# Query and key products of both mixers as one product of 512 columns, with later turns and a new end of the second mixer

## The reference, cut to what matters

```python
def rmsnorm(x, g):
    y = xf * lax.rsqrt(jnp.mean(xf * xf, axis=-1, keepdims=True) + EPS)
    return (y * g.astype(jnp.float32)).astype(x.dtype)

def dsw_mixer(h, w_qkv, q_gain, k_gain, w_o, rel_bias):
    qkv = (h @ w_qkv).reshape(B, S, 3, G, Hg, HEAD_DIM)
    q = rmsnorm(qkv[:, :, 0], q_gain)
    k = rmsnorm(qkv[:, :, 1], k_gain)
    v = qkv[:, :, 2]
    ...            # per group of 8 heads: windowed attention with a bias, softmax over the three groups
    return o.astype(h.dtype) @ w_o

def moba_mixer(h, w_qkv, q_gain, k_gain, w_o, rel_bias):
    qkv = (h @ w_qkv).reshape(B, S, 3, H, hd)
    q = rmsnorm(qkv[:, :, 0], q_gain).transpose(0, 2, 1, 3)
    k = rmsnorm(qkv[:, :, 1], k_gain).transpose(0, 2, 1, 3)
    ...            # causal attention per head with a bias
    return o.astype(h.dtype) @ w_o

for i in range(DEPTH):     # DEPTH = 2
    u = rmsnorm(h, norm_mix[i])
    h = h + (dsw_mixer if i == 0 else moba_mixer)(u, ...)
    h = h + sq_relu_mlp(rmsnorm(h, norm_ffn[i]), ffn_w1[i], ffn_w2[i])
```

## Time and profile before

| | us |
|---|---|
| median of 3 runs | 1662.42 (1661.85 to 1662.98) |
| profiled execution, its own time | 1662.12 |
| its span | 1660.2 |
| TensorE busy | 1625.4 (98% of the span) |
| VectorE busy | 1240.5 (75%) |
| ScalarE busy | 972.9 (59%) |

### The profile page before, as it was taken

The page is one execution under the profiler, slowest core; times in us unless marked ns, Lnnn a source line. Parts: engine busy times, 40 slices in busy tenths (PEclk is TensorE's granted clock), DMA queues, the critical chain, the costliest instruction groups (busy, mean ns, idle before and its releaser), DMA issues.

```text
span 1660.2 us, 27613 instructions
## 1 busy us (share of the span) xinstructions
PE 1625.4 (98%) x11068; PEld 1478.9 (89%) x11068; DVE 1240.5 (75%) x1766; ACT 972.9 (59%) x1381; POOL 309.5 (19%) x307
## 2 busy tenths in 40 slices
PE   8999999999999999999999999999899999999997
PEld 6988888898888889998999999999898888888886
DVE  5565786665658666998875554799888898988897
ACT  6556675346656634555554443555558677776675
POOL 1331553123217402143120002132120000000000
PEclk9999999999999999999999999999999999999999
DMA  8632545455335554533435444543429898988983
GB/s 294 233 109 101 178 178 203 180 205 175 113 128 192 178 203 181 183 136 131 150 122 187 174 178 178 172 150 128 167 94 343 333 353 335 340 333 331 352 342 127
DMA packets 50197, 339.76 MB, mean 205 GB/s; under 512 B 5575, under 2 KB 7839, under 8 KB 10351
## 3 DMA queue, kind: packets, MB, share of 16 engines
q1 hardware_dynamic: 47344, 328.79, 54.3%
q0 software_dynamic: 2720, 9.13, 1.8%
HBM read 336.76 MB, written 1.13 MB: 204 GB/s over the span
## 4 chain that ended last, share of the span: by engine, by line
PE 88%; DVE 5%; ACT 3%; issue 1%; POOL 1%; DMA 1%; SPq 0%; DVEq 0%; POOLq 0%; ACTq 0%
PE bank L528 12%; PE bank L502 8%; PE bank L504 8%; PE bank L503 8%; PE bank L526 7%; PE bank L956 5%; PE bank L957 5%; PE bank L958 5%; PE bank L659 3%; PE bank L661 3%; PE bank L660 3%; PE bank L989 2%; PE bank L988 2%; PE bank L987 2%; DVE wl L1698 2%
## 5 line engine op out<-in xcount | busy, mean ns | idle before, releaser
L1698 DVE TENSOR_TENSOR wl<-stg,wh 128x2048 fp32r<-128x2048 f32 x310 | 712.4, 2302 | 212.1 <-ACT wh L1198 210.2
L1198 ACT ACTIVATE wh<-stg 128x2048 fp32r<-128x2048 f32 x310 | 592.7, 1912 | 185.6 <-PE bank L958 82.4
L502 PE MATMUL bank<-xx,wh 128*128 128x272 f32 (+1 forms) x810 | 235.2, 290 | 2.5 <-DVE xx L2123 2.5
L504 PE MATMUL bank<-xx,wl 128*128 128x272 f32 (+1 forms) x810 | 232.5, 287 | 0.0
L503 PE MATMUL bank<-xx,wh 128*128 128x272 f32 (+1 forms) x810 | 232.3, 287 | 0.0
L528 PE MATMUL bank<-xx,wh 128*128 128x512 f32 x448 | 159.7, 396 | 0.0
L502 PEld LDWEIGHTS bank<-xx,wh 128*128 128x128 f32 x810 | 152.4, 188 | 5.1 <-issue 3.5
L503 PEld LDWEIGHTS bank<-xx,wh 128*128 128x128 f32 x810 | 153.6, 190 | 0.0
L504 PEld LDWEIGHTS bank<-xx,wl 128*128 128x128 f32 x810 | 152.3, 188 | 0.0
L528 PE MATMUL bank<-H,wh 128*128 128x512 f32 x434 | 151.3, 390 | 0.0
L956 PE MATMUL bank<-wh,GH 128*128 128x512 f32 (+3 forms) x400 | 147.5, 369 | 0.0
(11 more groups left out here) (374 smaller groups left out, 3507.6 us busy)
## 6 DMA issues: line engine op xcount, KB each, us to landing
stg<-in_w SPq DMA_DIRECT2D x310, 1024.0 KB, 4.8
BT<-bias_scratch POOLq DMA_DIRECT2D x3, 1024.0 KB, 11.2
BT<-bias_scratch POOLq DMA_DIRECT2D x1, 2048.0 KB, 13.0
BB<-bias_scratch POOLq DMA_DIRECT2D x2, 1024.0 KB, 6.4
res<-in_x SPq DMA_DIRECT2D x1, 1024.0 KB, 5.8
stg<-in_w SPq DMA_DIRECT2D x2, 512.0 KB, 7.4
BB<-bias_scratch POOLq DMA_DIRECT2D x2, 512.0 KB, 7.1
out<-res SPq DMA_DIRECT2D x4, 256.0 KB, 3.0
```

The lines of the kernel that those rows point to most:

```text
L502: pe.matmul(out, wh, xh(kt), start=kt == 0, stop=False)
L504: ins = pe.matmul(out, wl, xh(kt), start=False, stop=kt == KT - 1)
L1198: act.activation(WH[u % NW][:, :], stg[u % NS][:, :], ACT.Copy).then_inc(*m.inc("w_high", u))
L1698: vec.tensor_tensor(WL[u % NW][:, :], stg[u % NS][:, :], WH[u % NW][:, :].bitcast(F32), ALU.subtract).then_inc(*m.inc("w_low_v", u))
```

## The change

For each group, query and key become one product: `query_key` takes 4 blocks of weights per kt and issues the three matmuls with 512 columns into one bank per token tile, query in columns 0 to 255 and key in 256 to 511. The weights are laid out for it on the host side (`head_tiles`). Half a kt (one token tile) is now one slot, so that slots, units and split points keep their numbers: slot 8 bi + 2 kt + tt. Both kinds are ready only at the end of the key's entry of `order`, so ACT's copies, POOL's squares and DVE's sums come as four tiles in a row behind entry bi of kind 1, and none behind kind 0 (ACT and DVE still split a unit at kt 0 there).

The tables move too. In the first mixer two turns come two slots later, (8, 7) to (9, 1), and one slot later, (16, 7) to (17, 0). In the second mixer all turns move: behind slot 1 of the entry that follows the values, and `order` ends with (3, 0), (3, 1), (2, 2), (3, 2), so that the last two value pairs stand behind the last keys. The plan that follows from these tables for the second mixer is: before, steps 0 to 7 in slots (3, 1) to (4, 7), 8 to 15 in (6, 1) to (7, 7), 16 to 23 in (9, 1) to (10, 7), 24 to 37 left over; after, steps 0 to 6 in (3, 3) to (4, 7) and 7 in (5, 1), 8 to 14 in (6, 3) to (7, 7) and 15 in (8, 1), 16 to 18 in (9, 3) to (9, 7), 19 to 21 in (10, 1) to (10, 5), 22 to 25 in (11, 1) to (11, 7), 26 to 37 left over. In the first mixer the plan stays as it is (steps 2 and 3 in (10, 2) and (10, 5), 4 and 5 in (11, 2) and (11, 5)). The early split ahead of step 26 goes.

```diff
-              turns={(3, 5): 0, (6, 5): 1, (8, 7): 2, (12, 5): 3, (15, 1): 4, (16, 7): 5},
+              turns={(3, 5): 0, (6, 5): 1, (9, 1): 2, (12, 5): 3, (15, 1): 4, (17, 0): 5},
...
-              order=QKV[:12], turns={(3 * gi + 2, 7): gi for gi in range(4)},
-              sums_at=(0, 7), ring=8, late=24, leads={24: 0, 25: 1, 27: 2, 29: 3, 31: 4, 33: 5, 36: 6}, tables={})]
+              order=QKV[:8] + [(3, 0), (3, 1), (2, 2), (3, 2)], turns={(3, 1): 0, (6, 1): 1, (9, 1): 2, (11, 1): 3},
+              sums_at=(0, 7), ring=8, late=24, leads={27: 0, 28: 1, 29: 2, 30: 3, 31: 4, 33: 5, 36: 6}, tables={})]
...
+                def products(out, kt, tt, wh, wl):
+                    pe.matmul(out, xh_t(kt, tt), wh, start=kt == 0, stop=False)
+                    pe.matmul(out, xl_t(kt, tt), wh, start=False, stop=False)
+                    return pe.matmul(out, xh_t(kt, tt), wl, start=False, stop=kt == KD - 1)
+
+                def query_key(bi, gi):
+                    bs = [bank(("qkv", l, gi, 0, tt), ("raw", (l, gi, 0, tt)), ("raw", (l, gi, 1, tt))) for tt in range(2)]
                     held.update(b for b, _ in bs)
                     for kt in range(KD):
-                        wh, wl = take(2)
+                        wh, wl = take(4)
...
+                            ins = products(PS[b][:, :], kt, tt, wh, wl)
...
+                            between(*divmod(bi * KD + 2 * kt + tt, KD))
...
+                for bi, (gi, kind) in enumerate(c["order"]):
+                    if kind == 0:
+                        query_key(bi, gi)
+                    elif kind == 2:
+                        value(bi, gi)
...
-                        ps = bank(("qkv", l, gi, kind, tt))[:, 0:256]
+                        ps = bank(("qkv", l, gi, kind, tt))[:, kind % 2 * 256:kind % 2 * 256 + 256]
...
-                    if l == 0 and bi == 0:
+                    if kind == 0:
                         continue
-                    if l == 0 and bi == 1:
-                        evac(*c["order"][0])
+                    if kind == 1:
+                        evac(gi, 0)
                     evac(gi, kind)
                 for i in rest:
-                    if l == 1 and i == 26:
-                        sp.one_ahead()
                     step(i)
...
-                    for k1 in ((0, 1) if l == 0 and bi == 1 else (kind,) if kind < 2 else ()):
+                    for k1 in ((0, 1) if kind == 1 else ()):
...
-                    if kind < 2:
-                        for tt in range(2):
-                            i = kind * 2 + tt
-                            w.wait_ge(*m.of("raw", (l, gi, kind, tt)))
+                    if kind == 1:
+                        for i in range(4):
+                            k1, tt = divmod(i, 2)
+                            w.wait_ge(*m.of("raw", (l, gi, k1, tt)))
...
```

More of the change, by code:

```diff
@@ L643, in transposes, with between @@
                             ins.then_inc(*m.inc("group", ("qk", l, gi, kind, tt)))
-                for bi, (gi, kind) in enumerate(c["order"]):
-                    sem = "v_out" if kind == 2 else "raw"
-                    bs = [bank(("qkv", l, gi, kind, tt), (sem, (l, gi, kind, tt))) for tt in range(2)]
+                def between(bi, kt):
+                    if (bi, kt) in plan:
+                        step(plan[bi, kt])
+                    if (bi, kt) == c["sums_at"]:
+                        if l == 0:
+                            w.wait_ge(*m.of("consts_in"))
+                        square_sums(st, 2 if l == 0 else 1)
+                    if (bi, kt) in c["tables"]:
+                        bias_table(c["tables"][bi, kt])
+                    if (bi, kt) in c["turns"]:
+                        transposes(c["turns"][bi, kt])
+                def products(out, kt, tt, wh, wl):
[4 more added lines that the diff above has]
+                    bs = [bank(("qkv", l, gi, 0, tt), ("raw", (l, gi, 0, tt)), ("raw", (l, gi, 1, tt))) for tt in range(2)]
                     held.update(b for b, _ in bs)
                     for kt in range(KD):
-                        wh, wl = take(2)
+                        wh, wl = take(4)
                         if bi == 0:
@@ L657, in mixer @@
                                 vacant(old)
[L658 to L661, removed]
+                                m.bank["qkv", l, gi, 1, tt] = b
+                            ins = products(PS[b][:, :], kt, tt, wh, wl)
@@ L662, in mixer @@
                             if kt == KD - 1:
-                                ins.then_inc(*m.inc("group", ("qkv", l, gi, kind, tt)))
+                                ins.then_inc(*m.inc("group", ("qkv", l, gi, 0, tt)))
+                                m.also("group", ("qkv", l, gi, 1, tt))
+                                if tt == 1:
+                                    m.also("group", ("unit", at[0] // UT - 1))
+                            elif tt == 1 and unit_over():
+                                ins.then_inc(*m.inc("group", ("unit", at[0] // UT - 1)))
@@ new lines, in query_key, with value @@
+                            between(*divmod(bi * KD + 2 * kt + tt, KD))
+                    let_go(*sorted(b for b, _ in bs))
+                def value(bi, gi):
+                    bs = [bank(("qkv", l, gi, 2, tt), ("v_out", (l, gi, 2, tt))) for tt in range(2)]
+                    held.update(b for b, _ in bs)
+                    for kt in range(KD):
+                        wh, wl = take(2)
+                        for tt in range(2):
+                            b, old = bs[tt]
+                            if kt == 0:
+                                vacant(old)
+                            ins = products(PS[b][:, 0:256], kt, tt, wh, wl)
+                            if kt == KD - 1:
+                                ins.then_inc(*m.inc("group", ("qkv", l, gi, 2, tt)))
@@ L664, in mixer @@
                         if kt == KD - 1:
                             m.also("group", ("unit", at[0] // UT - 1))
[L666 to L673, removed]
@@ L674, in mixer @@
-                        if (bi, kt) in c["turns"]:
-                            transposes(c["turns"][bi, kt])
-                    let_go(*sorted(b for b, _ in bs))
+                        between(bi, kt)
+                    let_go(*sorted(b for b, _ in bs))
+                for bi, (gi, kind) in enumerate(c["order"]):
[3 more added lines that the diff above has]
+                        value(bi, gi)
                 name, KT, lead, old = f"wo{l}", c["HG"] // 2, [], []
@@ L2465, in mixer @@
                             step(plan[bi, kt])
-                    if kind < 2:
-                        for tt in range(2):
-                            i = kind * 2 + tt
-                            w.wait_ge(*m.of("raw", (l, gi, kind, tt)))
+                    if kind == 1:
+                        for i in range(4):
+                            k1, tt = divmod(i, 2)
+                            w.wait_ge(*m.of("raw", (l, gi, k1, tt)))
                             if gi >= 1:
-                                w.wait_ge(*m.of("head_sum", (l, gi - 1, kind, tt)))
+                                w.wait_ge(*m.of("head_sum", (l, gi - 1, k1, tt)))
                             w.wait_ge(*m.of("rstd", st))
-                            pool.tensor_tensor(sqr[i], raw[i], raw[i], ALU.mult).then_inc(*m.inc("raw_sq", (l, gi, kind, tt)))
+                            pool.tensor_tensor(sqr[i], raw[i], raw[i], ALU.mult).then_inc(*m.inc("raw_sq", (l, gi, k1, tt)))
                     if l == 0 and bi == 3:
@@ L2628, in head_tiles @@
     t = w.reshape(k // P, P, 3, groups, 2, 2, P)
-    return np.concatenate([t[:, :, kind, mixer["groups"][gi][1], mixer["groups"][gi][2]].transpose(0, 2, 1, 3).reshape(-1, P, P)
-                           for gi, kind in mixer["order"]])
+    part = lambda gi, kind: t[:, :, kind, mixer["groups"][gi][1], mixer["groups"][gi][2]].transpose(0, 2, 1, 3)
+    return np.concatenate([(np.concatenate([part(gi, 0), part(gi, 1)], axis=1) if kind == 0 else part(gi, 2)).reshape(-1, P, P)
+                           for gi, kind in mixer["order"] if kind != 1])
 def token_tiles(w):
```

## The result

The changed kernel took 1672.44 us (median of 4 runs, 1670.93 to 1673.13), the kernel before 1662.13 (4 runs) beside it: 1.0064 of the time, 95% interval 1.0053 to 1.0076. That is slower by 0.64%; the prediction was 1675.0 us, in a range of 1665 to 1681.

The account below looks back on a forecast made before the run. TensorE was taken to set the time. Second-mixer waits 14.7, first mixer 1.6 and clock 3.4, less 3.0 at the second mixer's end and 3.8 for columns, gave +12.9 us on 1662.12: 1675.0 us, range 1665 to 1681.

Parts of the forecast that it names:

- The deciding step: Second mixer's products: steps' bias falls behind head norm and split on DVE, so TensorE waits 14.7 us together.
- r: Start of ACT's first copy for the second mixer's head norm, put at K + 1.6 us.
- K: End of a group's last key product in the second mixer; a late step's bias was put at K + 10.4 us.
- The waits, group by group: TensorE's waits in the second mixer: group 1 4.1 us, group 2 3.5, group 3 6.9, group 0 0.2.
- the 0.9 at (11, 3): Second mixer, group 3: the bank of job 22 waits 0.9 us behind a split, some 9 us after the 6.0 wait.
- The columns: Query and key products: 960 matmuls of 256 columns become 480 of 512, saving 3.8 us.
- The first mixer: First mixer: longer norm burst and later turns change TensorE's waits by +1.6 us, bounds 0 and +3.5.
- The end: Second mixer's last steps: waits for QT 0.6 and bias 1.4 go, 1.0 of slow clock too: 3.0 us saved.
- The clock: Second mixer: two slow stretches of 1.7 us each behind long TensorE waits, +3.4 us, bounds 0 and 8.5.
- Rival 2: TensorE's waits come, clock stays up, engines that got ahead save 2 us more: +7.5 us, 1669.6; chance 0.24.
- Rival 3: Each of TensorE's five long waits brings a slow clock stretch of 1.7 us: +18.0 us, 1680.1; chance 0.11.
- Rival 1: Second mixer: TensorE reaches the banks late enough not to feel DVE's chain: -6.8 us, 1655.3; chance 0.08.

Follow-up runs that it names:

- The table of four: Wide-product kernels: turns as before, values as before 1659.65 us or behind the last keys 1659.77; turns two slots later, 1671.40 and 1672.44 (the changed kernel).
- steps at other slots: Changed kernel with the second mixer's steps in slots 1, 3, 4, 6, 7 of an entry in place of 1, 3, 5, 7: 1659.66 us.
- the split twice: Changed kernel with VectorE making the low half of one weight unit twice behind the second mixer's norms of groups 1 to 3: 1680.31 us.
- the kernel with the values back: Changed kernel with the second mixer's values, lead tiles and early split as before, turns still two slots later: 1671.40 us.
- the first four runs: The first four experiments, timed in rounds beside the kernel before, which took 1661.38 us there.

## Why the prediction was right

**The deciding step held.** The links of VectorE's chain came within 0.3 us of what was worked out: r at K + 1.9 (ScalarE's first copy at 433.66) for K + 1.6, the bias at K + 10.6 for K + 10.4. TensorE's own arrival was counted 0.5 to 0.8 us too early: it stands at K + 8.2, 9.2 and 4.9 in groups 1 to 3, for 7.7, 8.4 and 4.4, since the first product behind a step takes 0.1 us more than the others (432.58 to 432.81) and the odd step 0.68 us and not 0.5 (434.11 to 434.79). Moving the bias on VectorE alone took the loss away, and lengthening the chain by 2.3 lengthened the waits by 2.3.

**The waits, group by group.** Group 1: 2.4 and 0.7 for 2.7 and 1.4; group 2: 1.5 and 1.1 for 2.0 and 1.5; group 3: 5.7 for 6.0, and the 0.9 at (11, 3) did not come; group 0: none for 0.2. The sum is 11.4 us where the prediction had 14.7, inside its bounds of 9 to 19. The three long waits were right to 0.5 us. The waits for QT that follow in groups 1 and 2 were too long in the forecast for the same reason as the long ones: ScalarE's last copy ends at 399.28 and 427.50, K + 15.2 and 14.5 for 15.3 and 14.5, but TensorE comes at K + 14.5 and 13.5 for 13.9 and 13.0. Why the 0.9 did not come was not taken apart.

**What caused them** was named half. The prediction gave both table changes as reasons, the late turns and the values behind the last keys. The table of four shows that the turns alone make the loss, whichever place the values have; they only decide at which instruction TensorE then waits.

**The columns.** 480 x (0.235 - 0.229) = 2.9 us by the medians, for 3.8. The three matmuls per tile of the earlier trace rows (0.227) were the nearer form, but 0.002 too fast; nothing comes near the 0.20 us that would have refuted the step. One reading was not right: the view of the earlier trace rows also has two waits for a split of weights, 0.5 us ahead of the first product and 0.3, where the prediction says none. No term rests on it.

**The first mixer.** +1.6 less its share of the columns (288 of 480, 2.3) is -0.7; measured -1.29. With 288 x 0.006 = 1.7 of columns its waits cost 0.4 and not 1.6. The wait for zm behind the norm is there, 1.1 us for 0.8 of before and a predicted 2.0, and the wait for the POOL division fell from 1.6 to 0.7 (11 to 167 us):

```profile
PE bank L581 <- ACT QT L1295: 1.2, 2, 0.8
PE bank L658 <- DVE zm L1801: 1.1, 1, 1.1
...
PE bank L594 <- POOL Lm L2487: 0.7, 1, 0.7
```

With only the products wide its first to last product took 136.18 us, in the changed kernel 135.72. The new turns were not tried alone, and the seven kernels with wide products that have them take 135.48 to 136.06, so that a gain of the turns is not shown. What they change can be read: the wait of 1.3 us for the POOL division at 144.7 us has gone, and two for QT, of 0.4 and 0.8 us, have come.

**The end.** The waits for QT and for the early split's bias went, 2.0 as predicted, and the slow stretch with them. The late split costs nothing that shows. The rest of the 6.04 us by which the end is shorter is work that moved into the products.

**The clock** was mis-sized. Two slow stretches were predicted at 1.7 us each (+3.4), and 1.0 of the one of before to go: +2.4 together. In the mixers there is one, longer, in place of one. PEclk stands third from the end of the row:

```profile
441.00:448.00 7.00, 5.63 (x29) 4.77 (x30) 2.37 (x11) 2.41 (x9) 2.42 (x3) 0.51 0.46 150
```

It is 1.2 GHz from 441 us, within the wait, to 447.9; TensorE works in it for 5.5 us, so that 2.7 are lost, against 1.7 in the earlier trace rows: +1.0 net. A second one, outside the mixers (1185.1 to 1188.5 us), stands behind waits that the kernel before has too, at full clock there. Of the ten profiles of this document five have one at this place (the changed kernel, the wide products alone, the tables alone, steps at other slots, the split twice), five have none: it belongs to the execution and not to the change. It does not cost its 1.7 us either: the part behind the second mixer is 0.56 longer, since two waits of 0.5 us each for ScalarE, which the kernel before has at 1190 and 1191 us, do not come.

**The sum** stood at +12.9 on the profiled execution and +8.8 was measured on it (span to span), +10.3 between the medians. The waits gave 3.3 less, the clock in the mixers 1.4 less, the first mixer 1.2 less, the columns 0.9 less of a gain; that makes 7.9. The two mixers measured +8.45 (9.74 - 1.29), of which a wait of 0.4 for PTm in the products, in no term of the sum, is most of the 0.55 left over; what is left beyond the mixers is mostly the 0.56 behind them, less 0.3 at the start and the end. All terms but the columns err to the same side, so that the sum is not right by errors that cancel. Rival 2 had 1669.6 and its condition, waits at full clock, was met for two of three long waits: the truth lies between forecast and rival 2. The median of 1672.44 is in the forecast's band, the profiled execution, at 1670.93, just outside it, in rival 2's. Rival 3 fell (no slow stretch behind 2.4 and 1.5 us), though with the split made twice every wait for zm had one. Rival 1 fell. The Trainium skill's section cited for rival 3 ("TensorE: Matmul & The Clock Gate", "What's actually happening") holds for the 5.7 us wait, and no more than sometimes for the shorter ones, as the last part shows.

## What to carry to other kernels

A table that places work on one engine also places it in the queues of the others: before a step is moved by a slot or two, look where it falls relative to the longest burst on each in-order engine, for the step that comes behind the burst carries all of it. An engine that is busy for half of a stretch can set the time one for one at such a place, and the cheap repair is to reorder the engine that is late (or to fit the steps ahead of the burst), which here gave back all of the loss. Of the wider product's gain the reordering left 0.2 us at an equal clock, and the steps ahead of the burst 1.5. When a step is moved out of the way, count which one now stands last behind the burst, and who asks for it.

## What the hardware showed beyond that

The clock does not answer to a wait of a given length in the same way each time. In the kernel with the values back, TensorE twice waited 2.38 us in the same place of two groups, after the same last products:

```profile
395.92 0.50 PE L658 MATMUL bank<-wh,xx 128*128 128x512 f32 x1 [2.38 <-DVE zm L1803]
...
424.88 0.70 PE L658 MATMUL bank<-wh,xx 128*128 128x512 f32 x1 [2.38 <-DVE zm L1803]
```

Behind the first the clock stayed at 2.4 GHz, behind the second it fell to 1.2 for 3.4 us:

```profile
396.00:400.00 4.00, 3.82 (x23) 3.14 (x23) 0.94 (x1) 4.00 (x9) 0.93 (x1) 1.00 0.74 262
425.00:429.00 4.00, 4.00 (x17) 3.68 (x18) 0.98 (x1) 4.00 (x9) 0.93 (x1) 0.57 0.73 266
```

Likewise the waits of the earlier trace rows were followed by a slow stretch in the kernel before and by none with the wide products alone, whose window reads 1.00:

```profile
443.50:468.00 24.50, 20.74 (x173) 16.46 (x172) 14.03 (x45) 14.34 (x43) 0.93 (x1) 1.00 0.24 87
```

And it differs between executions of one kernel: of the 25 executions of the kernel before beside the first four runs, ten had a mean granted clock of 0.999 and took 1659.62 to 1661.55 us, six had 0.996 and took 1662.66 to 1664.06. So a term of 1.7 us in a sum like this is in part a matter of chance, and the profiled execution shows only one draw of it.
